# Strassen's scheme for the up projections of an encoder's feed-forward stage: 16 of 22 feature tiles, parts of 6, 8 and 8

## The reference

```python
h = _rmsnorm(x, g_ffn[l])
z = _dwconv_centred(h @ w_up[l], conv_w[l], conv_b[l])   # 3 taps over the tokens
z_gate, z_val = jnp.split(z, [D_FF], axis=-1)            # D_FF = 2816: 22 tiles of 128 each
x = x + (jax.nn.silu(z_gate) * z_val) @ w_down[l]
```

## Time and profile before

| | before |
|---|---|
| median of 3 runs | 1104.08 us (1103.99 to 1104.28) |
| span of the profiled execution | 1102.4 us |
| PE busy | 1092.6 us, 99% |
| DVE, ACT, POOL busy | 531.0, 484.7, 464.8 us |
| granted PE clock | 0.999 of full speed |

### The profile page before, as it was taken

One profiled execution on the slowest core, in us unless ns is written; L12 is line 12 of the kernel. 1 busy time (PEld: TensorE's weight loads), 2 busy tenths in 40 slices (PEclk: granted clock), 3 DMA queues, 4 the chain that ended last, 5 costly groups with the idle time before them and its releaser, 6 DMA issues.

```text
span 1102.4 us, 16315 instructions
## 1 busy us (share of the span) xinstructions
PE 1092.6 (99%) x5328; PEld 905.8 (82%) x5328; DVE 531.0 (48%) x816; ACT 484.7 (44%) x656; POOL 464.8 (42%) x202
## 2 busy tenths in 40 slices
PE   9999999999999999999999999999999999999997
PEld 7788888888888888888878888888888888888886
DVE  5726755655215551255536368456541355314545
ACT  7835444454225441344557344346432454313451
POOL 5334234344534443544634332435444444444450
PEclk9999999999999999999999999999999999999999
DMA  8222223232222222222522212222332322232222
GB/s 301 93 96 78 68 76 105 78 109 100 96 95 94 97 96 95 96 96 97 180 97 81 91 63 74 95 77 96 115 95 76 115 96 95 79 117 91 96 77 78
DMA packets 33607, 108.79 MB, mean 99 GB/s; under 512 B 3984, under 2 KB 6800, under 8 KB 33552
## 3 DMA queue, kind: packets, MB, share of 16 engines
q1 hardware_dynamic: 32848, 107.03, 29.2%
q10 hardware_dynamic: 704, 1.07, 0.3%
HBM read 105.98 MB, written 2.10 MB: 98 GB/s over the span
## 4 chain that ended last, share of the span: by engine, by line
PE 97%; DVE 1%; DMA 1%; ACT 0%; POOL 0%; SPq 0%; issue 0%; DVEq 0%
PE acc L1044 28%; PE acc L1045 28%; PE acc L1046 28%; PE acc L1170 3%; PE acc L1171 3%; PE acc L1172 3%; PE side L1140 1%; PE side L1258 1%; PE side L1242 1%; DMA x<-xT 1%; PE side L1248 1%; PE side L1221 1%; DVE arena L1019 1%; PE side L1201 1%; PE acc L1132 0%; PE acc L1121 0%
## 5 line engine op out<-in xcount | busy, mean ns | idle before, releaser
L339 POOL TENSOR_TENSOR w_lo<-w_raw,w_hi 128x1024 fp32r<-128x1024 f32 x188 | 453.4, 2416 | 600.6 <-ACT w_hi L348 600.6
L1044 PE MATMUL acc<-xg_hi,w_hi 128*128 128x512 f32 x864 | 338.8, 392 | 0.0
L1045 PE MATMUL acc<-xg_lo,w_hi 128*128 128x512 f32 x864 | 336.3, 389 | 0.0
L1046 PE MATMUL acc<-xg_hi,w_lo 128*128 128x512 f32 x864 | 336.2, 389 | 0.0
L348 ACT ACTIVATE w_hi<-w_raw 128x1024 fp32r<-128x1024 f32 x190 | 200.0, 1057 | 255.2 <-PE acc L1046 219.2
L1044 PEld LDWEIGHTS acc<-xg_hi,w_hi 128*128 128x128 f32 x864 | 162.2, 188 | 35.8 <-issue 2.0
L1046 PEld LDWEIGHTS acc<-xg_hi,w_lo 128*128 128x128 f32 x864 | 162.2, 188 | 33.9
L1045 PEld LDWEIGHTS acc<-xg_lo,w_hi 128*128 128x128 f32 x864 | 162.2, 188 | 33.5 <-issue 0.5
L1044 PE MATMUL acc<-feat_hi,w_hi 128*128 128x512 f32 (+1 forms) x492 | 188.9, 384 | 0.0
L1045 PE MATMUL acc<-feat_lo,w_hi 128*128 128x512 f32 (+1 forms) x492 | 188.8, 384 | 0.0
L1046 PE MATMUL acc<-feat_hi,w_lo 128*128 128x512 f32 (+1 forms) x492 | 188.8, 384 | 0.0
(11 more groups left out here) (131 smaller groups left out, 803.2 us busy)
## 6 DMA issues: line engine op xcount, KB each, us to landing
w_raw<-slabs SPq DMA_DIRECT2D x190, 512.0 KB, 3.3
outT<-arena SPq DMA_DIRECT2D x7, 256.0 KB, 2.3
ln_sb<-ln_gb SPq DMA_DIRECT2D x2, 512.0 KB, 7.7
w_raw<-slabs SPq DMA_DIRECT2D x4, 128.0 KB, 4.6
x<-xT ACTq DMA_DIRECT2D x2, 256.0 KB, 4.6
x<-xT SPq DMA_DIRECT2D x2, 256.0 KB, 5.9
x<-xT ACTq DMA_DIRECT2D x1, 512.0 KB, 7.2
w_raw<-slabs SPq DMA_DIRECT2D x2, 256.0 KB, 6.9
```

What stands on the lines that cost most here:

```text
L339: pool.tensor_tensor(w_lo[:, w], w_raw[:, w], w_hi[:, w].bitcast(F32), ALU.subtract).then_inc(lo_done, 1)
L1044: pe.matmul(out, wh, ah, start=first, stop=False)
L1045: pe.matmul(out, wh, al, start=False, stop=False)
L1046: return pe.matmul(out, wl, ah, start=False, stop=last)
```

## The change

The weights of four up tiles (2 features, gate and value) and the activations are cut in 2 x 2: A by gate and value and by even or odd channel tiles, B by channel parity and token halves (H = 256). Strassen's scheme in Winograd's form makes the four blocks of C out of seven products instead of eight:

- weight sums S1 = A21 + A22, S2 = S1 + A11, S3 = A11 + A21, S4 = A12 + S2 (sums only: the signs of the scheme are put into the token combinations and the last steps);
- token combinations T1 to T4, made once a layer out of `x` by DVE (`combine`, `t_low`) during the first part, rounded by ACT;
- products in PE's order: S1 T1, A11 B11, A12 B21, S2 T2, A22 T4, S3 T3, S4 B22. Bank 1 collects A11 B11, then S2 T2, then S3 T3, and ACT copies it out after the first two (`copy`), with S1 T1 and S3 T3 copied too.

The parts are now 6, 8, 8. The first part (6 feature tiles) is made as before; the other 16 tiles are 4 rounds in each of two parts in each of two layers. S1, S3 and S4 are made by transfers that add into SBUF, issued by POOL in its own list (`add_s1`, `add_s3`, `add_s4`), the first two from HBM, the third from SBUF; S2 by DVE (`add_s2`). Four further DVE steps a round (`add_c11` and so on) combine the products, and the scaling then runs in place. The down products of a part take three banks together, six features first.

In the rows of order below, `sides` is the tensor with the four PSUM banks y, `u_copy` one of the copies, `arena` a large SBUF tensor of many uses, `mixer_sb` the mixer's weights whose room the sums use.

POOL, first place: the end of its loop over slabs before, and one round, the second of a part, now (S1 and A11 are the first row).

```diff
+            def add_s1(L, p, s):
+                pool.wait_ge(a21_loaded[s % 2], 16 * ((L * QUADS + p * KP + s) // 2 + 1))
+                pool.dma_start(raw1[s % 2], block_of(L * NS + first_slab(p, s) + 3),
+                               accum_op=ALU.add).then_inc(s1_added[s % 2], 16)
+            def add_s3(L, p, s):
+                low_done(L * NU + first_unit(p, s) + A11_)
+                pool.wait_ge(s2_done, L * QUADS + p * KP + s + 1)
+                pool.dma_start(raw0[s % 2], block_of(L * NS + first_slab(p, s) + 1),
+                               accum_op=ALU.add).then_inc(s3_added[s % 2], 16)
+            def add_s4(L, p, s):
+                low_done(L * NU + first_unit(p, s) + A12_)
+                pool.dma_start(raw2[s % 2], s2_raw, accum_op=ALU.add).then_inc(s4_added[s % 2], 16)
+            def low_quad(L, p, s):
+                n = L * NU + first_unit(p, s)
+                low(n + S1_, raw1[s % 2])
+                low(n + A11_, raw0[s % 2])
+                add_s3(L, p, s)
+                if s < KP - 1:
+                    add_s1(L, p, s + 1)
+                low(n + A12_, raw2[s % 2])
+                add_s4(L, p, s)
+                low(n + S2_, s2_raw)
+                low(n + A22_, raw(3))
+                low(n + S3_, raw0[s % 2])
+                low(n + S4_, raw2[s % 2])
...
+                def high(unit, source):
+                    j = unit % RING
+                    act.wait_ge(acc_ready, L * NU + (unit + 1 - RING))
+                    act.activation(w_hi[:, j * SLAB:(j + 1) * SLAB], source, ACT.Copy).then_inc(hi_done, 1)
...
+                def quad_step(p, s):
+                    if s:
+                        centre(p, s - 1, 1)
+                    high_s2(p, s)
+                    if s:
+                        centre(p, s - 1, 0)
+                    copy(p, s, S1_, 2 + s % 2, p5_copy)
+                    high_a22(p, s)
+                    if s:
+                        centre(p, s - 1, 2)
+                        silu(p, s - 1, 0)
+                        centre(p, s - 1, 3)
+                    copy(p, s, A11_, 1, p1_copy)
+                    high_s3(p, s)
+                    if s:
+                        silu(p, s - 1, 1)
+                        feat_high(p, s - 1, 0)
+                    high_s4(p, s)
+                    if s:
+                        feat_high(p, s - 1, 1)
+                        act.wait_ge(c12_added, quad_at(p, s))
+                    copy(p, s, S2_, 1, u2_copy)
+                    if s < KP - 1:
+                        high_s1(p, s + 1)
+                        high_a11(p, s + 1)
+                    else:
+                        high_down(p, 0)
+                        high_down(p, 1)
+                    copy(p, s, S3_, 1, u3_copy)
+                    if s < KP - 1:
+                        high_a12(p, s + 1)
+                    else:
+                        high_down(p, 2)
...
+                def add_s2(p, s):
+                    count = 16 * (L * (QUADS // 2)) + 16 * ((p * KP + s) // 2 + 1)
+                    dve.wait_ge(s1_added[s % 2], count)
+                    dve.wait_ge(a11_loaded[s % 2], count)
+                    if p or s:
+                        before = p * KP + s - 1
+                        dve.wait_ge(s4_added[before % 2], 16 * (L * (QUADS // 2)) + 16 * (before // 2 + 1))
+                        dve.wait_ge(lo_done, L * NU + (first_unit(before // KP, before % KP) + S2_ + 1 + RING))
+                    dve.tensor_tensor(s2_raw, raw1[s % 2], raw0[s % 2], ALU.add).then_inc(s2_done, 1)
+                def add_c11(p, s):
+                    dve.wait_ge(acc_ready, L * NU + (first_unit(p, s) + A12_ + 1))
+                    dve.wait_ge(copied, quad_at(p, s) * 4 + 2)
+                    dve.tensor_tensor(y_of[:, 0, :, 0, :], halves(acc[0][:, :]), halves(p1_copy),
+                                      ALU.add).then_inc(c11_added, 1)
+                def add_c12(p, s):
+                    dve.wait_ge(acc_ready, L * NU + (first_unit(p, s) + S4_ + 1))
+                    dve.tensor_tensor(y_of[:, 0, :, 1, :], halves(acc[2 + s % 2][:, :]), halves(u2_copy),
+                                      ALU.add).then_inc(c12_added, 1)
+                def add_c22(p, s):
+                    if s:
+                        dve.wait_ge(feat_ready, L * NF + (KT + FIRST_TILES + p * KT + 2 * s))
+                    dve.wait_ge(copied, quad_at(p, s) * 4 + 4)
+                    dve.scalar_tensor_tensor(out=y_of[:, 1, :, 1, :], in0=halves(acc[1][:, :]), scalar=-1.0,
+                                             in1=halves(p5_copy), op0=ALU.mult,
+                                             op1=ALU.subtract).then_inc(c22_added, 1)
+                def add_c21(p, s):
+                    dve.scalar_tensor_tensor(out=y_of[:, 1, :, 0, :], in0=halves(acc[3 - s % 2][:, :]), scalar=-1.0,
+                                             in1=halves(u3_copy), op0=ALU.mult,
+                                             op1=ALU.subtract).then_inc(c21_added, 1)
...
+                def convolve(p, s, between):
+                    add_c12(p, s)
+                    scale(p, s, 0)
+                    taps(p, s, 1)
+                    scale(p, s, 2)
+                    taps(p, s, 0)
+                    scale(p, s, 3)
+                    taps(p, s, 2)
+                    between()
+                    gate(p, s, 0)
+                    taps(p, s, 3)
+                    quad_low(p, s, 0)
+                    gate(p, s, 1)
+                    quad_low(p, s, 1)
+                def quad_step(p, s):
+                    if s:
+                        convolve(p, s - 1, (lambda: add_s2(p, s + 1)) if s < KP - 1 else (lambda: None))
+                    else:
+                        add_s2(p, 1)
+                    add_c11(p, s)
+                    add_c22(p, s)
+                    add_c21(p, s)
+                    scale(p, s, 1)
...
+                def up_products(p, s):
+                    n = first_unit(p, s)
+                    quads = L * QUADS + p * KP + s
+                    own, other = 2 + s % 2, 3 - s % 2
+                    def free(added, tile):
+                        if s:
+                            pe.wait_ge(added, quads)
+                        else:
+                            pe.wait_ge(x_done, L * NX + RING + (p + 1) * KT + tile + 1)
+                    def has_copied(n_copies):
+                        pe.wait_ge(copied, quads * 4 + n_copies)
+                    free(c21_added, 6)
+                    if p == 0 and s == 0:
+                        pe.wait_ge(t1_ready, L + 1)
+                        pe.wait_ge(t_ready, (L + 1) * KP)
+                    product(own, n + S1_, t1, True)
+                    free(c22_added, 5)
+                    product(1, n + A11_, b11, True)
+                    free(c11_added, 4)
+                    product(0, n + A12_, b21, True)
+                    has_copied(2)
+                    product(1, n + S2_, t2, False)
+                    free(c12_added, 7)
+                    product(other, n + A22_, t4, True)
+                    has_copied(3)
+                    product(1, n + S3_, t3, False)
+                    product(own, n + S4_, b22, False)
+                def down_products(p, tiles):
+                    n = first_unit(p, KP)
+                    quads = L * QUADS + (p + 1) * KP
+                    feats = L * NF + KT + FIRST_TILES + p * KT
+                    bank_free = (c11_added, c22_added, c21_added, c12_added)
+                    early = KT - 2
+                    for k, j in ([(k, j) for j in range(3) for k in range(early)]
+                                 + [(k, j) for k in range(early, KT) for j in range(3)]):
+                        if k == 0:
+                            slab_wait(n + j)
+                            pe.wait_ge(bank_free[j], quads)
+                        if j == 0:
+                            pe.wait_ge(feat_ready, feats + k + 1)
+                        last = three(acc[j][:, :], w_block(j, k * P), feat(k), k == 0, k == KT - 1)
+                        if k == KT - 1:
+                            last.then_inc(acc_ready, 1)
+                    for m in range(3, tiles):
+                        slab_wait(n + m)
+                        if m == 3:
+                            pe.wait_ge(bank_free[m], quads)
+                        else:
+                            pe.wait_ge(x_done, L * NX + RING + (p + 2) * KT + m - RING + 1)
+                        project(m % RING, feat)
```

520 lines of the change are left out of this document (395 added, 125 removed).

## The result

| | before | after |
|---|---|---|
| median | 1104.05 us (1103.99 to 1104.28) | 1119.05 us (1116.78 to 1119.95) |
| ratio | | 1.0133, 95% interval 1.0118 to 1.0147 |
| profiled execution, its span | 1104.1, 1102.4 | 1118.4, 1116.6 |
| TensorE busy | 1092.6 | 1081.9 |
| mean granted clock | 0.999 | 0.988 |

The forecast was 1094.2 us. The change made the kernel 15.0 us slower, and the span grew by 14.2. A part is one stretch of four Strassen rounds; the first and second lie in the first layer, the third and fourth in the second. Rounds are counted from 0.

The account below looks back on a forecast made before the run. TensorE was taken to bound the kernel. Span 1102.4 - 25.6 (products) + 0.2 (tail) + 0.7 (features late in the first part) + 14.8 (S2 loop stalls) = 1092.5, + 1.7 (span to median) = 1094.2 us; range 1081 to 1116.

Parts of the forecast that it names:

- What bounds the kernel: Whole kernel: TensorE, busy 1092.6 of 1102.4 us; less TensorE work saves time as long as no other engine becomes late.
- The products, -25.6 us: TensorE's Strassen rounds: 168 matmuls of 256 columns take 20.16 us instead of 21.76, 1.60 saved in each of 16 rounds.
- Rival (d): TensorE's 256-column matmuls: weight loads not prefetched for long; 0.1295 us each would eat the gain, 0.188 cost 183 us; chance 0.04.
- Issue and landing: GpSimd's adding transfers: 1.2 us an issue, landing 4.5 us after issue, from 2.9 to 7.
- d = 1.0: GpSimd's adding transfers: an issue of 1.0 us instead of 1.2, the rest unchanged, would give 1090.0 us.
- The loop that decides, +14.8 us: Rounds 1 and 2: S4's landing holds S2, gates, features, copy of U2 and product S3; 3.7 us in each of four parts.
- X = 10.05 and 12.2: VectorE: when S2 ends in rounds 1 and 2, in us into the round, giving stalls of 0.75 and 2.95 us.
- rival (b): S4's sum lands after S3's residue has begun, so S2 waits another pass: stalls 35.6 us, 1115 us; chance 0.26 with (c).
- The lock: VectorE with two SBUF operands waits for GpSimd's pass to end; in the loop only S2, 1.25 us, GpSimd's next residue stopping.
- covered by 0.4: C21 must leave its bank before the next S1 product: VectorE done at 19.7 us, due 20.16, so no wait.
- (a): GpSimd's adding transfers are cheap, issue 0.33 to 0.7 us, landing near 3: stalls 1.6 to 6.8 us, 1081 to 1086; chance 0.18.
- (c): GpSimd as plain throughput bound: costs time above an issue of 1.3 us, all the gain at 1.9; chance 0.26 with rival (b).

Follow-up runs that it names:

- run 3: Two kernels against the changed one: S4's transfer adds from HBM instead of S2's tile, 1108.5 us; S2's operation left out except once a layer, 1093.0 us.
- runs 3 and 4: Besides run 3: the changed kernel with A12's residue and S4's transfer ahead of S3's and the next S1's transfers on GpSimd, 1139.6 us.
- run 2: Changed kernel with S2 moved on VectorE from between taps and first gate to behind both gates and feature differences; 1090.7 us, 0.9878.
- the last kernel of run 8: Changed kernel with S2 last in VectorE's round, S2's residue on VectorE instead of GpSimd, copy of P1 ahead of all three centres on ScalarE; 1106.5 us.
- the first kernel of run 8: Changed kernel with S2 as VectorE's last step of a round and S2's residue computed by VectorE instead of GpSimd; 1128.5 us.

## Why the prediction was wrong, by its steps

**What bounds the kernel.** Right: TensorE did, and the warning that others become late came true.

**The products, -25.6 us.** Right; 80.63 us a part without sums. Rival (d) is refuted. The Trainium skill's 2.5 ns a matmul ("TensorE: Matmul & The Clock Gate", section "Wait — 56ns, not 53.3ns?") does not hold for these matmuls at 256 columns, in 16 whole rounds either: it is 13.3 ns each.

**Issue and landing.** Assumed 1.2 us for an issue of GpSimd's and 4.5 us from issue to landing. Measured: 0.88 to 1.19 us, with 0.6 between two starts, so the issue was too dear. The landing, from part 6 of the page (KB each, median us to landing), was too cheap:

```profile
w_raw<-slabs POOLq DMA_DIRECT2D x16, 512.0 KB, 5.8
...
arena<-slabs POOLq DMA_DIRECT2D x16, 512.0 KB, 6.4
...
w_raw<-mixer_sb POOLq DMA_DIRECT2D x8, 512.0 KB, 6.4
mixer_sb<-mixer_sb POOLq DMA_DIRECT2D x8, 512.0 KB, 5.6
```

These groups mix the transfers. By themselves S4's sums land 6.1 us after their issue in the median (4.5 to 7.5), S1's 7.4 (5.8 to 8.4). This is a mis-sized term. The bound of 7 us held S4's median, the value of 4.5 did not; I built it from a plain load that had the engines to itself, and in the parts they are 56 to 62% busy. The 1090.0 that stands beside the forecast for d = 1.0 comes out at 1089.6 by its own working. The Trainium skill ("DMA: Bandwidth & Descriptors", section "Anatomy of one DMA — SWDGE (gpsimd) path") gives 2.0 us plus the bytes at 436 GB/s for one transfer, by my estimate 3.2 us here; the rows are at about twice that, for transfers that add and run beside others.

**The loop that decides, +14.8 us.** The chain was right link by link: S4's sum, S2, gates, features, copy of U2, product S3, in rounds 1 and 2 and not in 0 and 3. Its tail of 5.1 us was 4.7. What failed is the place where S2 gets in. The working let it in behind GpSimd's residue of A22, at X = 10.05 and 12.2. In the change seven of the eight S2s of rounds 1 and 2 end 1.08 or 1.09 us behind the residue of S3, one pass later: rival (b), at part of its price. There were two reasons. In round 1 the landing missed the gap between the two passes: in the second part it came at 451.49, and GpSimd had begun the residue of S3 at 451.16. Round 1 cost 7.5 us for a forecast of 3.0, and without the landing, in run 3, nothing. In round 2 of the first part the two passes follow without such a gap, and a landing after 4.6 us would not have helped, as run 3 shows. Round 2 cost 13.1 us for 11.8. That round 1 of the first part paused 0.76 us, for a forecast of 0.75, is luck: S2 ended 10.7 us into the round, not 10.05, and the shorter tail made up for it, and the other three had 2.54, 1.68 and 2.54. The arithmetic also had S2 wait for one transfer alone; in runs 3 and 4 S1's sum stands in the same wait.

**The lock.** The prediction says that for S2 "POOL's next residue must stop". The earlier trace rows show VectorE getting in behind the first of two passes, and the working let S2 in at the next end of a pass everywhere. In round 0 S2 waited through the rest of a run of five, 9.9 us, and C21, "covered by 0.4", was late by 1.7 and 2.8 us, 4.5 in all. The Trainium skill ("SBUF — State Buffer", section "Who interferes with whom") says that a VectorE instruction with two inputs in SBUF contends with a GpSimd instruction that reads SBUF, and calls what they share an exclusive lock. The rows agree for one pass: S2 ends about its own time behind it.

**The clock.** Missing from the sum: the prediction priced a stall at its idle time alone. Seven pauses of 2.5 to 4.0 us each cost 1.7 us more, some 12 us, nearly as much as all forecast stalls, and with the refilling of TensorE the largest single error. Without this the change would have ended near 1107. The forecast's own stall of 2.95 us was longer than the 2.54 that brought it here.

**Adding up.** -25.6 in the products; +20.6 for the copy of U2 (forecast 14.8); +4.5 for C21 (0); +13.1 clock and refill (0); +1.6 outside the parts (0.9). Sum +14.2, the difference of the spans. That is 24.1 us above the forecast span: 13.1 clock and refill, 5.8 copy of U2, 4.5 C21, 0.7 outside.

**Rivals.** (a) is refuted by the landings; its issue of 0.33 to 0.7 us was nearer than mine, by the 0.6 us between two starts. (b) had the mechanism and the right neighbourhood, 1115, but by longer pauses (35.6 us for 20.6) and without the clock, so its number is partly luck. (c), GpSimd's throughput, isn't what decided here: moving S2 alone won 28.3 us with the same load on GpSimd. It does have a part in the last 10 us. How they divide among the three queues is left open, since no run relieved all three.

## What to carry to other kernels

A step that waits for a transfer should stand where nothing that the bounding engine needs stands behind it on its in-order queue; here that place alone was worth 28 us, and moving it beat both kernels. Before pricing such a wait, list every semaphore in it, and every lock behind it: with the latest transfer gone, another transfer still held the step, and behind that a pair of passes, which alone kept one pause at 3.99 us. A pause of the bounding engine is to be priced with its slow clock, so many short waits are cheaper than a few long ones of the same sum.

## What the hardware showed that I had not expected

- VectorE, with two operands in SBUF, took 9.9 us for a 1.22 us step while GpSimd ran passes back to back (12.5 and 12.6 in the first kernel of run 3). With GpSimd standing still the same step took 1.22 us. It got in between two passes where the next was listed from at most 0.07 us before the end of the one before (25 of 25), and never where it was listed from 0.16 to 0.34 us before it (30 of 30).
- An adding transfer of 512 KB issued by GpSimd landed 5.6 to 6.4 us later in the median of each group (4.5 to 8.4 in all), and its issue takes 0.88 to 1.19 us. GpSimd's next pass is listed at 2.7 us behind one issue and 3.1 behind two, for 2.4; part of that is overlap of the records, since passes listed at 2.7 in a row start 2.4 apart.
- The granted clock fell to the 1.2 GHz level behind each pause of 2.5 us or more in the change, and behind none of 0.76 to 1.68 us. Each fall cost 1.7 us (31% of 5.5 us), so it lasted about 3.4 us. Between these it did not go by length alone: behind a pause of 2.40 us in run 2 (888 to 893 us) the clock was 0.66, behind one of 2.51 in the last kernel of run 8 (849 to 854) 1.00, behind one of 1.8 in the first kernel of run 8 (370 to 375) 0.70.

```profile
888.00:893.00 5.00, 3.54 (x17) 3.55 (x18) 4.71 (x8) 2.39 (x3) 4.55 (x4) 0.66 0.66 105
```

```profile
849.00:854.00 5.00, 4.12 (x34) 4.12 (x35) 0.32 (x1) 3.67 (x6) 4.58 (x2) 1.00 0.11 28
```

```profile
370.00:375.00 5.00, 3.98 (x22) 3.99 (x23) 4.18 (x7) 4.21 (x7) 3.01 (x2) 0.70 0.32 105
```

- Each pause costs TensorE about 0.16 us beyond the listed idle time: the matmul before it shows 0.28 us instead of the 0.12 between starts.
